# Bias rows written into PSUM by ScalarE in every group of experts, not only in those of two blocks

## What is computed

```python
def expert_block(args):                    # xe: up to 128 tokens, e: their expert
    xe, e = args
    gu = xe @ w_gate_up[e] + b_gate_up[e]  # [128, 1024] @ [1024, 2048]
    gate, up = jnp.split(gu, 2, axis=-1)
    gate = jnp.minimum(gate, SWIGLU_LIMIT)
    up = jnp.clip(up, -SWIGLU_LIMIT, SWIGLU_LIMIT)
    act = gate * jax.nn.sigmoid(SWIGLU_ALPHA * gate) * (up + 1)
    return act @ w_down[e] + b_down[e]     # [128, 1024] @ [1024, 1024]
```

## Time and profile before

| | |
|---|---|
| median of 3 runs | 2291.99 us (2290.93 to 2295.94) |
| the profiled execution | 2300.91 us |
| its span, first to last instruction | 2299.2 us |
| expert stage in it | from about 712 us to the end |
| TensorE busy | 2178.1 us, 95% of the span |
| VectorE busy | 1756.1 us, 76% |
| ScalarE busy | 1358.2 us, 59% |
| GpSimd busy | 815.7 us, 35% |
| moved by DMA | 603.19 MB, 262 GB/s over the span |

### The profile page before, as it was taken

The page is one execution under the profiler, slowest core; times in us unless marked ns, Lnnn a source line. Parts: engine busy times, 40 slices in busy tenths (PEclk is TensorE's granted clock), DMA queues, the critical chain, the costliest instruction groups (busy, mean ns, idle before and its releaser), DMA issues.

```text
span 2299.2 us, 37071 instructions
## 1 busy us (share of the span) xinstructions
PE 2178.1 (95%) x10302; PEld 1799.2 (78%) x10303; DVE 1756.1 (76%) x2165; ACT 1358.2 (59%) x1859; POOL 815.7 (35%) x804
## 2 busy tenths in 40 slices
PE   5999997888977899999999999999999999999997
PEld 4678885776865788888888888888888888888885
DVE  5683422676775799977799977788999779798897
ACT  4332211575325577766667766676777666677675
POOL 2263003885134234432224422142444322144241
PEclk9899998899988999999999999999999999999999
DMA  7233205883336899997789988797999878899794
GB/s 268 87 115 138 60 19 121 239 230 109 115 125 235 285 367 365 379 355 271 267 295 374 384 295 269 237 358 270 387 376 371 324 265 310 286 359 386 258 382 159
DMA packets 299090, 603.19 MB, mean 262 GB/s; under 512 B 24720, under 2 KB 46240, under 8 KB 295392
## 3 DMA queue, kind: packets, MB, share of 16 engines
q1 hardware_dynamic: 270912, 528.95, 64.1%
q0 software_dynamic: 27072, 69.40, 10.9%
q10 hardware_dynamic: 1056, 4.19, 0.5%
HBM read 563.71 MB, written 44.53 MB: 265 GB/s over the span
## 4 chain that ended last, share of the span: by engine, by line
PE 65%; DMA 2%; issue 1%; DVE 0%; POOL 0%; POOLq 0%; DVEq 0%; ACT 0%; ACTq 0%
PE psum L2255 60%; PE psum L2194 2%; PE psum L2237 2%; PE psum L2202 2%; DMA d_xg<-xn_d,d_entry 1%; DMA d_entry<-list_d 1%; POOL d_spare L1846 0%; POOL d_roww L1903 0%; DVE d_wlo L2073 0%; DVE d_yst L2126 0%; DVEq L1738 0%; ACT d_whi L1930 0%; POOLq L1689 0%; POOLq L1690 0%; POOLq L1842 0%
## 5 line engine op out<-in xcount | busy, mean ns | idle before, releaser
L2073 DVE TENSOR_TENSOR d_wlo<-d_raw,d_whi 128x1024 fp32r<-128x1024 f32 x578 | 676.7, 1219 | 127.7 <-ACT d_whi L1930 125.4
L1930 ACT ACTIVATE d_whi<-d_raw 128x1024 fp32r<-128x1024 f32 x578 | 579.8, 1054 | 62.7 <-PE psum L2255 49.7
L2255 PE MATMUL psum<-d_whi,d_xthi 128*128 128x512 f32 x1152 | 455.5, 395 | 6.1 <-issue 6.1
L2255 PE MATMUL psum<-d_whi,d_xtlo 128*128 128x512 f32 x1152 | 450.2, 391 | 0.0
L2255 PE MATMUL psum<-d_wlo,d_xthi 128*128 128x512 f32 x1152 | 449.9, 391 | 0.0
L1835 POOL DMA_INDIRECT out_dram<-d_yst,d_dest x49 | 149.7, 3055 | 665.2 <-DVE d_yst L2126 660.5
L2073 DVE TENSOR_TENSOR d_wlo<-slab,d_whi 128x1024 fp32r<-128x1024 f32 x292 | 343.8, 1219 | 21.6 <-ACT d_whi L1930 19.2
L1930 ACT ACTIVATE d_whi<-slab 128x1024 fp32r<-128x1024 f32 x292 | 292.3, 1054 | 7.7 <-PE psum L2255 6.1
L2255 PEld LDWEIGHTS psum<-d_whi,d_xthi 128*128 128x128 f32 x1152 | 217.3, 189 | 51.8 <-issue 8.0
L2255 PEld LDWEIGHTS psum<-d_whi,d_xtlo 128*128 128x128 f32 x1152 | 217.1, 188 | 46.3
L2255 PEld LDWEIGHTS psum<-d_wlo,d_xthi 128*128 128x128 f32 x1152 | 217.4, 189 | 43.6
(11 more groups left out here) (351 smaller groups left out, 4010.8 us busy)
## 6 DMA issues: line engine op xcount, KB each, us to landing
slab<-in_w_gate_up_dram SPq DMA_DIRECT2D x144, 1024.0 KB, 8.4
d_raw<-in_w_gate_up_dram SPq DMA_DIRECT2D x144, 1024.0 KB
d_raw<-in_w_down_dram SPq DMA_DIRECT2D x144, 1024.0 KB
b_wp<-in_w_ada_dram POOLq DMA_DIRECT2D x16, 1024.0 KB, 9.4
slab<-in_w_in_dram SPq DMA_DIRECT2D x12, 1024.0 KB, 5.4
d_bias_rows<-in_b_gate_up_dram SPq DMA_DIRECT2D x12, 1024.0 KB
d_bias_rows<-in_b_down_dram SPq DMA_DIRECT2D x12, 512.0 KB
a_xin<-in_x_dram ACTq DMA_DIRECT2D x2, 2048.0 KB
```

The costliest lines, as they stand in the source:

```text
L1930: nc.scalar.activation(whi[n % NW][:, part, :], raw[n % NRAW][:, part, :], ACT.Copy).then_inc(whi_ok, 1)
L2073: nc.vector.tensor_tensor(wlo[n % NW][:, part, :], raw[n % NRAW][:, part, :], whi[n % NW][:, part, :].bitcast(F32), ALU.subtract).then_inc ...
L2255: mm = nc.tensor.matmul(to, m_[:, KH * h + k, :], w_[n % NW][:, k, :], start=(h == 0 and k == 0 and q == 0 and not loaded), stop=(h == 1 a ...
```

## The change

In groups of one block the bias of slabs 1 to 5 is no longer added by a matmul; it is preset by ScalarE, as in groups of two blocks. The parts:

1. TensorE: the matmul of `pick` and `bhl` falls away for slabs 1 to 5 of a one-block group, and its first matmul on each of them waits for `preset` and no longer for the engines that empty the bank.
2. ScalarE: five instructions of 128 x 512 are added to a one-block group, and with them waits that were there for two-block groups only, the one for the bias rows among them.
3. SyncE: the bias rows are loaded for every group. Slab 0's 512 columns are left out, so that a load is 128 x 1536 and 128 x 1024 float32 (1280 KiB), where it was 128 x 2048 and 128 x 1024 (1536 KiB).
4. At the start, the first load of bias rows is issued between the weight loads of halves 2 and 3, not ahead of the wait for the first tokens.

The core of the diff:

```diff
                 def load_bias(e):
-                    for cols, src in ((slice(0, 2 * F), a["b_gate_up"][0]), (slice(2 * F, 2 * F + D), a["b_down"][0])):
-                        sp.dma_start(bias_rows[:, cols], src[bass.ds(e, 1), :].broadcast_to([P, cols.stop - cols.start])
+                    for at, src in ((SL, a["b_gate_up"][0, :, SL:]), (2 * F, a["b_down"][0])):
+                        width = src.shape[1]
+                        sp.dma_start(bias_rows[:, at:at + width], src[bass.ds(e, 1), :].broadcast_to([P, width])
                                      ).then_inc(bias_in, 16)
-                def bias(e, g, blocks):
+                def bias(e, g):
                     sp.wait_ge(preset, PRE_CRED + PRE * g)
-                    if blocks == 1:
-                        sp.sem_inc(bias_in, 32)
-                    else:
-                        load_bias(e)
+                    load_bias(e)
-                load_bias(0)
...
                 load(0, 0, 2)
+                load_bias(0)
                 load(0, 0, 3)
...
-                def bias_first(g, j):
+                def bias_first(g, j, blocks):
...
+                    if j in (3, 5):
+                        act.wait_ge(sg_ok, pair_count(g, j // 4, 1, 1))
                     one = 1.0 if j < GU and j % 2 else 0.0
-                    for b, share in enumerate((1.0, 0.5)):
+                    for b, share in enumerate((1.0, 0.5)[:blocks]):
...
-                        if blocks == 2 and n in BIAS_STEP:
-                            bias_first(g, BIAS_STEP[n])
+                        if n in BIAS_STEP:
+                            bias_first(g, BIAS_STEP[n], blocks)
...
-                    loaded = blocks == 2 and j > 0
+                    loaded = j > 0
                     if h == 0 and loaded:
-                        pe.wait_ge(preset, PRE_CRED + PRE * g + 2 * (j - 1) + b + 1)
+                        pe.wait_ge(preset, PRE_CRED + PRE * g + 2 * (j - 1) + (b + 1) * sh)
```

More of the change, by code:

```diff
@@ L1768, in body @@
                             with sp.If(g > 0):
-                                bias(e, g, blocks)
+                                bias(e, g)
                         load(e, g, n)
-                def bias(e, g, blocks):
+                def bias(e, g):
                     sp.wait_ge(preset, PRE_CRED + PRE * g)
-                    if blocks == 1:
-                        sp.sem_inc(bias_in, 32)
-                    else:
-                        load_bias(e)
+                    load_bias(e)
                 def load_bias(e):
-                    for cols, src in ((slice(0, 2 * F), a["b_gate_up"][0]), (slice(2 * F, 2 * F + D), a["b_down"][0])):
-                        sp.dma_start(bias_rows[:, cols], src[bass.ds(e, 1), :].broadcast_to([P, cols.stop - cols.start])
+                    for at, src in ((SL, a["b_gate_up"][0, :, SL:]), (2 * F, a["b_down"][0])):
+                        width = src.shape[1]
+                        sp.dma_start(bias_rows[:, at:at + width], src[bass.ds(e, 1), :].broadcast_to([P, width])
                                      ).then_inc(bias_in, 16)
-                load_bias(0)
                 sp.sem_inc(wlo_ok, RAW_CRED)
@@ L1789, in _ @@
                 load(0, 0, 2)
+                load_bias(0)
                 load(0, 0, 3)
                 sp.wait_ge(bhl_ok, 2)
-                groups(sp, body)
+                groups(sp, body, wants_two=False)
                 g = total(sp)
@@ L1985, in bias_first @@
                         act.wait_ge(up_ok, UP_CRED + pair_count(g, 0, 1, 1))
+                    if j in (3, 5):
+                        act.wait_ge(sg_ok, pair_count(g, j // 4, 1, 1))
                     one = 1.0 if j < GU and j % 2 else 0.0
-                    for b, share in enumerate((1.0, 0.5)):
+                    for b, share in enumerate((1.0, 0.5)[:blocks]):
                         nc.scalar.activation(psum[:, 2 * (j % 3) + b, :], bias_rows[:, bias_at(j):bias_at(j) + SL],
-                                             ACT.Copy, bias=one * share, scale=share).then_inc(preset, 1)
+                                             ACT.Copy, bias=one * share, scale=share).then_inc(preset, 2 // blocks)
                 def body(e, g, blocks, read_next):
@@ L1995, in body @@
                     else:
-                        act.sem_inc(preset, PRE)
                         act.sem_inc(xthi_ok[1], 2)
@@ L2237, in bias @@
                         mm = nc.tensor.matmul(to[0:ROWS[b], :], pick[:, 0:ROWS[b]], bhl[:, at:at + SL], start=False, stop=last)
-                        if j == (GU + DN - 1 if blocks == 1 else 0) and b == blocks - 1:
+                        if b == 1:
                             mm.then_inc(pick_free, 1)
@@ L2258, in half @@
                                                   skip_group_check=loaded)
+                            if blocks == 1 and n == 2 and k == 0 and q == 0:
+                                mm.then_inc(pick_free, 1)
                         if b == blocks - 1 and k % 2 == 1 and counted(n, k // 2):
```

## The result

| | before | after |
|---|---|---|
| median of 7 runs, taken side by side | 2294.76 us (2290.93 to 2298.53) | 2309.75 us (2302.88 to 2317.54) |
| profiled execution, its span | 2300.91, 2299.2 us | 2306.04, 2304.2 us |
| the 24 one-block groups in it, sum | 870.4 us | 888.7 us |

After to before is 1.0065 (1.0044 to 1.0086): 15 us slower. Where the 5 us come from, by stretches of the two traces: one-block groups +18.4, the start of the expert stage -8.7, the part ahead of the stage (which the change does not touch, so it differs from run to run) -5.4, the rest +0.7.

The account below looks back on a forecast made before the run. Inside runs of one-block groups TensorE (35.88 us) and DMA (35.7) were taken as bounds within 1 us. Waits of 48 less a gain of 27 gave +21, plus 3 for the clock: +24, 2316 us, range 2288 to 2336.

Parts of the forecast that it names:

- DMA engines become the bound inside a run: Runs of one-block groups: with bias rows, DMA sets the pace, 4.15 us a group over TensorE's new pace.
- A group's transfers need 35.7 us before and 38.9 after: One-block groups: 35.7 us of DMA time, plus 3.2 for bias rows, gives 38.9 (38.2 to 39.3).
- TensorE's saving of 1.13 us a group, 27.2 in all: One-block groups: five fewer bias matmuls at 0.2267 us each let TensorE finish in 34.75 us; 24 groups.
- ScalarE's writes are hidden: One-block groups: five writes of 0.58 us raise ScalarE from 26.9 to 29.8 us, covered under 34.75; nothing charged.
- The delay goes through slab 1's bank, and TensorE stalls before the third matmul half: Inner one-block groups: late bias rows delay slab 1's preset, so TensorE idles some 4 us.
- The second group of a run has no wait: Second groups just meet their bias; 12 groups from the third on pay 4.15 us each, 48 in sum.
- The clock, +3: Half clock behind the last waiting group of each of five long runs, 0 to 17 us; 3 added.
- The start, 0 (-1 to +3): First loads: first gather up to 1 us earlier, half 3 some 3 us later but hidden; taken as 0.
- The transfers are hidden: Rival, chance 0.08: one-block transfers fit within 34.75 us with bias rows, so TensorE's saving comes through; 2265 us.
- The lead absorbs it: Rival, chance 0.17: loads ahead absorb 5 to 7 us in each of five long runs; about 2278 to 2288, up to 2297.
- The clock falls in every pause: Rival, chance 0.20: TensorE's new pauses of some 4 us each drop the clock; +38, 2330 us.
- The profile of the changed kernel as foretold: Signs: bias matmuls 168 to 48, writes 120 to 240, 28 MB more DMA, inner groups 38.2 to 39.3 us.

Follow-up runs that it names:

- three slabs: The changed kernel, but one-block groups preset only slabs 3, 4 and 5 and load 768 KiB of bias rows, awaited at step 3: 2279.90 us, 0.992 of before.
- the rows alone: The kernel before, but every group loads the 1280 KiB of bias rows; one-block groups keep their bias matmuls, ScalarE waits at step 7: 2301.37 us, 1.0016.
- two-slab kernel: The changed kernel, but one-block groups preset only slabs 4 and 5 and load 512 KiB of rows, awaited at step 5: 2286.17 us, 0.9952 of before.

## Why the prediction was right or wrong

**Forecast 2316, measured 2309.75, inside the range and on the side named.** Several steps that lead there were off, and in part made up for each other: that the number came so near is in good part luck.

- *DMA engines become the bound inside a run*: right. Three kernels with the wait in three places come to 37.8 to 38.1 us in the run shown, where the clock does not fall, at 395 to 399 GB/s.
- *A group's transfers need 35.7 us before and 38.9 after*: mis-sized, at most 34.99 (the group without bias matmuls) and 37.8. The step that failed is "I take 35.7, near the upper end, since the share dips nowhere". The 35.0 that I worked out as a lower bound from bytes was the better guess. The row's 1.04 is a sum of packets' durations, which overlap: 1.05 goes with 35.15 us of the same work as well as with 37.8 of more. The 3.2 us for the rows was not measured by itself; 37.8 less 34.99 says that it is at least 2.8.
- *TensorE's saving of 1.13 us a group, 27.2 in all*: mis-sized, 0.73 (851.2 against 870.4: 19 us in all, of which 2.9 are group 1, where the half clock went). Of the missing 0.40 us, 0.17 are idle time, waits of up to 0.3 us for `d_act` since VectorE has 34.1 us of work in 35. The other 0.23 stayed in TensorE's busy time, which fell from 35.88 to 34.98 and not to 34.75; why was not tried, so a bias matmul was worth (35.88 - 34.98) / 5 = 0.18 us there and not the 0.2267 of a mean over twelve starts.
- *ScalarE's writes are hidden*: nearly. They take 0.16 us a group, 4 in all. With the writes behind the splits (three slabs) the group was 0.13 us shorter, so it is the splits, which VectorE waits for, that they hold up.
- *The delay goes through slab 1's bank, and TensorE stalls before the third matmul half*: wrong. "The lead of the weights doesn't help, because the new gate on slab 1 lies before it" was the false step. ScalarE's write of slab 1 ended at 1691.38 + 0.60 = 1691.98, 5.0 us into the group at 1686.99, and TensorE needed slab 1 at 25 matmuls, 5.67 us: in time, and late but once, by 0.3 us, in all of after. The margin is 0.7 us: with the write behind the split, TensorE did stand there, 11 times. I had looked at the first waiter and its nearest consumer, and had disposed of "behind those VectorE" with 34.0 us of work in 38.9. In 37.8 us, with 3.2 of it idle, there is no room to make up.
- *The second group of a run has no wait*: wrong, 37.25 us. VectorE has 1 us of spare a group, so the first wait already counts. There are 17 inner groups that pay, not 12, but each pays less: (888.7 - 851.2) / 17 = 2.2 us, where I had 4.15 x 12. The loss is 37.5 us instead of 48, the gain 19 instead of 27, the net of the groups +18.4 where I had +21.
- *The clock, +3*: the reason given was right, the size too large. Of the eleven stalls of 2.2 us (the "1.9 us" of the prediction, from start to start of matmuls, is 1.5 us by this measure) seven were without effect. Four times the clock fell to 0.50 for 3.4 us right behind one, as here (stretch as in the earlier trace rows, then the matmul whose wait came before it):

```profile
1225.40:1228.80 3.40, 3.26 (x10) 2.78 (x11) 3.40 (x5) 2.05 (x3) 0.00 (x0) 0.50 1.05 408
```

```profile
1225.54 1.12 PE L2201 MATMUL psum<-ident,d_act 128*128 128x128 f32 x4 [2.24 <-DVE d_act L2092]
```

  Such a group takes 39.3 to 40.4 us instead of 37.8, but the group behind it is shorter by nearly as much: 39.38 + 36.59 us at 1724.81, 39.31 + 36.25 at 1197.35, against 2 x 37.8. While TensorE runs at half clock the transfers go on at 408 GB/s, and the next wait shrinks, as the prediction says of drops inside a run. A drop cost less than 1 us. The Trainium skill (TensorE: Matmul & The Clock Gate, HAM oscillation — how this bites in real kernels) would have it fall in every tile's wait; in this trace it fell in four of the eleven groups with a stall of 2.2 us.
- *The start, 0 (-1 to +3)*: wrong by size and by place. I looked at the loads alone, and took their order for nothing; they are worth 2 to 4 of the 8.7 us. The other 6.1 us, and 2.4 of half clock in group 1, came from a branch of TensorE whose 6.11 us stood in the earlier trace rows with "issue" as its releaser, that is with no cause. I had used that row for the clock alone. Without these 8.5 us the result would have been about +24, the forecast's number, reached by other parts.
- *Rivals.* "The transfers are hidden" fell with the rows alone. "The lead absorbs it", which I put at 0.17, is what happens once the wait for the rows is moved: that kernel took 2294.65 us, in the upper part of its 2278 to 2297. "The clock falls in every pause" fell.
- *The profile of the changed kernel as foretold*: 48 bias matmuls, 240 writes, 28.3 MB more, first groups 35.3, and 35.7 in the runs of one (said: 34.9 to 35.3): right or nearly. Inner groups 37.8 (said: 38.2 to 39.3) and the idle place: wrong.

The prediction set the Trainium skill's 358 GB/s against a row of 409. That page's section Measured (HBM→SBUF, 128 partitions, SWDGE, issued from GpSimd) says, a step further on, that 358 holds with both cores of a pair streaming and gives 425 for one alone. The row, 409 GB/s, is of a core alone and lies near the latter, so the other figure had no place in the estimate.

**What stays open.** That the long branch is TensorE fetching code that lies too far ahead is argued, not shown: the kernels show that it goes with the length of the program (164 matmuls and more in the body, or 163 and 12 instructions added), and no row shows a fetch. Why it is 6.3 us in two kernels, 5.0 and 4.4 in two, and in the two-slab kernel a pause of 5.35 us with no long branch, no run tells. Nor does any run separate the DMA engines from the queue or the memory behind them: what is shown is that transfers set the pace, at some 397 GB/s a group.

## What to carry to other kernels

Trading matmul time for bytes pays only up to the spare of the DMA engines, and a summed DMA share just above 1 does not say that there is none: here one slab's rows cost an estimated 0.64 us of transfers for 0.18 us of TensorE, 1 us of spare and the loads ahead carried three slabs, and five were too many. A wait on an in-order engine must be followed to every consumer behind it, and charged first to the one with the least spare (VectorE, 34.1 of 35 us), not to the nearest; and it belongs behind the work that the others need. A pause with the releaser "issue" in the profile of before is a term to be explained before anything is estimated around it, since an edit that only shortens the program may remove it.

## What the runs showed of the hardware

- A conditional branch into a body that TensorE had not run before took 4.4 to 6.3 us in four kernels, 0.3 to 0.4 in the others, and was followed by up to 6.8 us at half clock. The median of the 48 was 208 ns, the shortest 77. The Trainium skill (Advanced Engine Details and Errata, Control Flow Timing) gives about 108 ns for a compare-and-branch, between these two, and says nothing there of long ones.
- An instruction of TensorE that only increments a semaphore, twelve in a row between matmuls, cost some 0.15 us of matmul time (1.7 us a group for the twelve).
- Over whole groups the transfers came at 391 to 400 GB/s with extra rows, also where TensorE still kept its pace (396 GB/s with three slabs, 35.58 us), and at 381 to 393 GB/s in the inner groups shown without them. The DMA share was 1.04 or 1.05 beside all of these: the summed share did not tell the two apart.
- After stalls of 2.2 us TensorE's clock fell to 1.2 GHz (granted clock 0.50) for 3.4 us four times, and stayed at 2.4 GHz after the seven others of that length.
